# 128 background weight tiles: their loads move from SyncE's DMA queue to GpSimd's

## The reference, cut to what matters

```
shift, scale, gate = split(silu(cond) @ ada_w[i] + ada_b[i], 3)      # for c and for c_ctx
h = rmsnorm(x, norm_w[i]) * (1 + scale) + shift
layer 0: q, k, v, g = h @ gla_w_in ; gated linear attention ; y = (rmsnorm(o) * silu(g)) @ gla_w_out
layer 1: q, k, v, g = h @ diff_w_in ; differential softmax attention ; y = (...) @ diff_w_out
x = x + gate * y
```

## Time and profile before

| | |
|---|---|
| median of 3 runs | 1594.27 us (1589.72 to 1596.06) |
| the profiled execution, its own time | 1593.43 us |
| its span, first to last instruction | 1591.5 us |
| mean granted TensorE clock | 0.993 of full speed |
| PE busy | 1551.6 us, 97% |
| DVE busy | 1162.1 us, 73% |
| ACT busy | 606.0 us, 38% |
| POOL busy | 2.2 us |
| DMA of SP's queue (q1) | 256.55 MB, 50.3% of 16 engines' span |
| DMA of ACT's queue (q10) | 11.22 MB, 2.3% |

### The profile page before, as it was taken

The page is one execution under the profiler, slowest core; times in us unless marked ns, Lnnn a source line. Parts: engine busy times, 40 slices in busy tenths (PEclk is TensorE's granted clock), DMA queues, the critical chain, the costliest instruction groups (busy, mean ns, idle before and its releaser), DMA issues.

```text
span 1591.5 us, 19504 instructions
## 1 busy us (share of the span) xinstructions
PE 1551.6 (97%) x7602; PEld 1252.6 (79%) x7602; DVE 1162.1 (73%) x1799; ACT 606.0 (38%) x934; POOL 2.2 (0%) x9
## 2 busy tenths in 40 slices
PE   5999999999999999999999999999999999999998
PEld 3567888788888878788887778888888888888886
DVE  4444878887787789677887687777676768575865
ACT  4222434433444433542222444343333424243642
POOL 0000000000000000000000000000000000000000
PEclk9899999999999999999999999999999999999999
DMA  9996344554544464344876244445444444352554
GB/s 351 370 320 215 120 139 133 177 162 118 171 136 151 114 221 147 106 132 156 263 235 214 85 139 159 158 145 178 153 138 157 157 160 148 103 170 78 159 179 143
DMA packets 177352, 269.02 MB, mean 169 GB/s; under 512 B 12534, under 2 KB 111024, under 8 KB 176588
## 3 DMA queue, kind: packets, MB, share of 16 engines
q1 hardware_dynamic: 170464, 256.55, 50.3%
q10 hardware_dynamic: 6796, 11.22, 2.3%
HBM read 265.60 MB, written 2.12 MB: 168 GB/s over the span
## 4 chain that ended last, share of the span: by engine, by line
PE 81%; DVE 10%; DMA 4%; ACT 2%; issue 1%; SPq 0%; ACTq 0%; DVEq 0%
PE bank L1172 62%; PE bank L1636 5%; DVE ada_w L1689 3%; DMA ada_w<-in_ada_w 3%; PE bank L1353 2%; PE bank L1104 2%; DVE w_lo L1664 2%; PE bank L1256 1%; PE bank L1257 1%; PE bank L1258 1%; DMA u<-in_ctx 1%; DVE work L1959 1%; ACT w_hi L641 1%; PE bank L1215 1%; DMA u<-in_ada_w 1%
## 5 line engine op out<-in xcount | busy, mean ns | idle before, releaser
L1172 PE MATMUL bank<-w_lo,acts_hi 128*128 128x512 f32 x1536 | 606.5, 395 | 12.5 <-DVE acts_lo L2088 3.4
L1172 PE MATMUL bank<-w_hi,acts_lo 128*128 128x512 f32 x1536 | 599.1, 390 | 0.0
L1172 PE MATMUL bank<-w_hi,acts_hi 128*128 128x512 f32 x1536 | 598.9, 390 | 0.0
L641 ACT ACTIVATE w_hi<-w_raw 128x1024 fp32r<-128x1024 f32 (+1 forms) x296 | 304.1, 1034 | 592.0 <-PE bank L1172 510.2
L1664 DVE TENSOR_TENSOR w_lo<-w_raw,w_hi 128x1024 fp32r<-128x1024 f32 (+1 forms) x296 | 349.8, 1192 | 175.4 <-ACT w_hi L641 175.0
L1172 PEld LDWEIGHTS bank<-w_lo,acts_hi 128*128 128x128 f32 x1536 | 288.8, 188 | 84.5 <-issue 12.9
L1172 PEld LDWEIGHTS bank<-w_hi,acts_lo 128*128 128x128 f32 x1536 | 288.7, 188 | 61.0
L1172 PEld LDWEIGHTS bank<-w_hi,acts_hi 128*128 128x128 f32 x1536 | 288.8, 188 | 57.2
L1689 DVE SCALAR_TENSOR_TENSOR ada_w<-ada_w,silu_p 128x1024 f32<-128x1024 f32 x210 | 261.5, 1280 | 36.7 <-DMA ada_w<-in_ada_w 34.0
L1172 PE MATMUL bank<-acts_hi,w_lo 128*128 128x512 f32 x208 | 83.6, 402 | 1.1 <-DVE acts_lo L1789 1.1
L1172 PE MATMUL bank<-acts_lo,w_hi 128*128 128x512 f32 x208 | 81.6, 392 | 0.0
(11 more groups left out here) (227 smaller groups left out, 1514.9 us busy)
## 6 DMA issues: line engine op xcount, KB each, us to landing
ada_w<-in_ada_w SPq DMA_DIRECT2D x146, 512.0 KB, 4.5
w_raw<-in_diff_w_in SPq DMA_DIRECT2D x256, 256.0 KB, 3.1
w_raw<-in_gla_w_in SPq DMA_DIRECT2D x64, 512.0 KB, 4.2
w_raw<-in_gla_w_out SPq DMA_DIRECT2D x32, 512.0 KB, 4.9
w_raw<-in_diff_w_out SPq DMA_DIRECT2D x32, 512.0 KB, 4.4
u<-in_ada_w SPq DMA_DIRECT2D x24, 512.0 KB, 9.4
w_raw<-in_gla_w_in SPq DMA_DIRECT2D x40, 256.0 KB, 3.5
w_raw<-in_gla_w_in SPq DMA_DIRECT2D x48, 128.0 KB, 4.1
```

The lines of the kernel that those rows point to most:

```text
L641: act.activation(w_hi[:, s, :, 0:w], raw[:, s, :, 0:w], ACT.Copy).then_inc(w_hi_ok, 1)
L1172: last = pe.matmul(bank[b][:], a, w, start=(k == 0 and i == 0), stop=(k == NK - 1 and i == 2))
```

## The change

All 128 `modulation_tile` requests leave SP's program and are issued by GpSimd, after its five memsets, one after the other, with the same waits, the same tiles, the same buffers and the same semaphores. SP keeps the layer-0 start-up loads of `ada_w` (line 473) and all pairs.

```
--- before.py
+++ after.py
@@ -473,18 +473,6 @@   (on SP)
-            def modulation_tile(m):
-
-                i, k = m // NK, m % NK
-                layer, part = ((0, 2), (1, 0), (1, 1), (1, 2))[i // 2]
-                if m < 2:
-                    sp.wait_ge(ada_used, QUADS)
-                else:
-                    sp.wait_ge(weighed, m - 1)
-                first = part * D + i % 2 * HALF_COLS
-                sp.dma_start(ada_tile[:, m % 2], io["ada_w"][layer][k * P:(k + 1) * P, first:first + HALF_COLS])\
-                    .then_inc(tile_in[m % 2], 16)
-
@@ -536,9 +524,6 @@   (on SP, in load_chunk)
-                    for m in range(WEIGHS):
-                        if c * PAIRS + p == (6 if m < 2 else WEIGH_AT[m - 2]):
-                            modulation_tile(m)
@@ -624,6 +609,21 @@   (on GpSimd, after its memsets)
+            def modulation_tile(m):
+
+                i, k = m // NK, m % NK
+                layer, part = ((0, 2), (1, 0), (1, 1), (1, 2))[i // 2]
+                if m < 2:
+                    pool.wait_ge(ada_used, QUADS)
+                else:
+                    pool.wait_ge(weighed, m - 1)
+                first = part * D + i % 2 * HALF_COLS
+                pool.dma_start(ada_tile[:, m % 2], io["ada_w"][layer][k * P:(k + 1) * P, first:first + HALF_COLS])\
+                    .then_inc(tile_in[m % 2], 16)
+
+            for m in range(WEIGHS):
+                modulation_tile(m)
```

## The result

The changed kernel takes 1599.83 us (median of 12 runs, 1597.34 to 1601.60) against 1593.09 (12 runs). The medians differ by 6.7 us; the ratio of the two sets of runs is 1.0046, 95% interval 1.0038 to 1.0053, that is 7.3 us more (6.1 to 8.4), and this is the figure used from here on. The prediction said 1602.9 us in a range of 1593 to 1618, and slower with a chance of 0.55. Time and sign are right, though by the prediction's own bound of 0.5%, 8.0 us, a loss of 7.3 us would still have been called "same". The working is not right: the lateness is a third of what I took, its price is about twice what my formula gives, and about half of it is paid where I saw cover. The profiled execution took 1598.33 us, 4.9 more than before's, so its trace shows about two thirds of the loss.

What follows compares the result with a forecast made beforehand. PE, busy 97%, was taken as the bound, with DVE the bound in five stretches where late tile landings reach PE. At d = 1.1, 1.1 + 2.2 + 3.1 + 1.1 + (0.9 + 2.2 - 2.0) = 8.6 us, forecast 1602.9 us, range 1593 to 1618.

Steps and rivals of the forecast that it cites:

- formula: Sum over five stretches where PE waits through DVE: 9d - 2.2 up to d = 0.8, above that 12d - 4.6.
- likeliest case: The forecast itself: d from 0.7 to 1.8, centre 1.1, time 1598 to 1612 us; chance 0.50.
- nearly hidden: Rival: d below 0.7, so -2.2 to +4.1 us, time 1592 to 1598; chance 0.20.
- d: Added time from the end of weigh(m - 2) to the landing of tile m; taken as 1.1 us, ends 0 and 4.1.
- The steps covered in `OUT0` and layer 1: `OUT0` before 835 us and layer 1: delay hidden by `low` running ahead and by DVE's idle time; no cost.
- 2d and 3d between the heads: 264 to 288 us: two late landings, 2d (2.2 us); 566 to 593 us: three, 3d - 0.2 (3.1 us).
- The own queue's 2.0 us at 847.86 us: Third chunk of `OUT0`: the 8.38 us tile passes a weight load ahead of it on SP's queue; -2.0 us.
- 189 to 211 and 620 to 641 us: Decays of head 0 and of head 3: one late landing on the chain each, d (1.1 us) apiece.
- Held up by DVE: Rival: GpSimd's request waits for DVE's current instruction to end; d = 2.3, 23.0 us, time 1617; chance 0.22.
- Nothing to pay for 128 requests on SP: Taking 128 requests, 43.5 us, off SP is worth nothing, since SP would have waited for the next `low` anyway.
- weights not late: Pairs land as before; the opposing rival had some 25 layer-0 pairs 0.3 us late, 8 us on top, 1611; chance 0.03.
- 5.6 us in all: PE's total wait in between its busy stretches, taken as the most an own queue could give back.

Runs made afterwards that it cites:

- slope's kernel: The changed kernel, with GpSimd clearing 512 columns of the free buffer ahead of each request; 1617.44 us, +24.4 against before.
- kernel of layer 1 alone: The kernel before, but the 30 tiles from 98 on are requested by GpSimd; 1593.82 us, +1.6 against before.
- the one with lateness on SP's queue: The kernel before, SP still requesting, but each request waits until GpSimd has cleared 384 columns of the free buffer; 1597.3 us, +4.1.
- the ring of four: The kernel before, its two tile buffers used as four half tiles of 512 columns, requested by SP, weighed half by half; 1587.09 us, ratio 0.9967.

## Why the prediction was right, point by point

The time came out inside the likeliest case (1598 to 1612), but of two errors that cancel, which is luck: by the measured lateness the case is the rival "nearly hidden" (d below 0.7, chance 0.20), whose time was 1592 to 1598. The table has the prediction's formula at the lateness that was measured, and the steps of PE's matmuls against those of before, in us:

| stretch (us of before) | formula, d = 0.33 | changed kernel | formula, d = 1.06 | slope's kernel |
|---|---|---|---|---|
| start, to 160 | 0 | +0.7 | 0 | +0.4 |
| 189 to 211 | 0.3 | -0.6 | 1.1 | 0.0 |
| 264 to 291 | 0.7 | +0.8 | 2.1 | +3.8 |
| 291 to 550 | 0 | 0 | 0 | +1.2 |
| 566 to 597 | 0.8 | +1.2 | 3.0 | +7.0 |
| 620 to 642 | 0.3 | -0.6 | 1.1 | -1.6 |
| 755 to 797 | 0 | +2.2 | 0 | +9.5 |
| 845 to 960 | -1.3 | +0.8 | 0.9 | +1.2 |
| layer 1 | 0 | +0.4 | 0 | +2.3 |
| sum | 0.8 | 4.9 | 8.1 | 23.8 |

The first row is not the change's: it arises ahead of 53 us, and the first tile is requested at 145 us.

- **The size of d** was the first error. I took 1.1, the middle between two rows of ACT's queue, and it is 0.33 (0.25 at the median). By the test that the prediction set itself, a median from request to landing that moves less than 0.4 (it went from 4.3 to 4.2), this step was wrong. The rows of ACT's queue held something else: the longer of them, 4.9 us, were loads amid a burst, and probably it was the burst that made them long. The Trainium skill's figures for the first byte ("DMA: Bandwidth & Descriptors", "Latency and other measured facts") gave 0.4 between the two paths; the packets show 0.22 to 0.26 from the request, and 0.5 with the later start. Either would have been the better choice.
- **The steps covered in `OUT0` and layer 1** were the second. The step that failed reads: "In `OUT0` before 835 us PE doesn't wait at all, since `low` runs up to four pairs ahead." PE not waiting shows that it has slack, not how much, and `low` is not all that PE takes from DVE. At line 1119 it waits for `weighed`, with 1.45 us to spare. A page of waits shows such an edge only once it is crossed. In the changed kernel this is the largest step, 2.2 us, and with tiles 67 to 82 undelayed the slope's kernel loses 6 to 8 us less. Not all of the 2.2 may be the change's: the kernel of layer 1 alone, with before's code there, is 0.7 us late at the same place in its execution. Layer 1, "a burst of up to four late tiles costs 4d = 4.4 us, which that idle time takes", crossed a smaller edge: 0.5 to 0.6 us at 1309 us, by traces alone, and so PE does wait in layer 1, which the prediction had named as a sign of being wrong. From 290 to 550 us the cover held at 0.33 us; at 1.06, close to the d = 1.1 that it was said to bear, it gave way by 1.2 us, 1.0 of it at 497 us.
- **2d and 3d between the heads** were too small in slope. At 1.06 us the steps are 3.8 and 7.0 in place of 2.1 and 3.0. Of these, 1.6 and 2.1 us are the clock behind the wait, which the prediction did not price; that leaves 2.2 and 4.8, so nearly 2 us of the second come from elsewhere, and I did not take them apart.
- **The own queue's 2.0 us at 847.86 us** did not come. The chain's tile there takes 8.48 us after, 8.38 before. It was not the weights ahead of it in line that made it slow, as the prediction thought it might be; a tile by GpSimd is slow amid the same loads. The same holds at 757.72 us (8.65): SP's request of that tile took 7.57 us before, 8.12 in the kernel of layer 1 alone and 8.73 in the one with lateness on SP's queue.
- **189 to 211 and 620 to 641 us** shrank instead of growing by d each. The second shrinks by 0.6 to 1.6 us in every kernel that I ran, by 1.4 in that of layer 1 alone, whose code is before's there, so it is no gain of the change; rather the profiled run of before was long there. The first goes from -0.9 to +0.7 us among the kernels and stands at +0.7 in that of layer 1 alone, so a d of 0.3 can't be seen in it; why it shows nothing at 1.06 us I leave open.
- **Held up by DVE** (0.22) was rightly second choice, and does not happen: 527 ns at the median, and a landing 0.1 us longer beside a `low` than without one (medians). With one-input instructions it would, at some requests. The 14 of line 1687 that the prediction names met none of the requests.
- **Nothing to pay for 128 requests on SP, and weights not late:** right. Behind the start-up no wait of PE or DVE names w_raw.
- **The waits of DVE for tiles** went up by 10 us, not 40, which is d again. PE still has no wait from 290 to 550 us: right.
- **"5.6 us in all"** was a misreading of PE's waits from 160 to 960 us. The same view holds 6.2 us more, 5.9 of it in these two lines, all behind 900 us at the change to layer 1:

```profile
PE bank L1172 <- DVE acts_lo L2088: 3.4, 2, 1.9
...
PE bank L1172 <- DVE v_lo L2174: 2.5, 1, 2.5
```

So 5.6 us was no bound on what an own queue could give back. And the 2.5 us take up lateness of PE: in the changed kernel they shrink to 1.0 (see the last section).

## What to carry to other kernels

Ask of a moved request not only what the queues do but how late the landing is behind what frees its buffer, and count how often such landings stand in series: the chain of the changed kernel passes fifteen where it passed eight, and at 16 to 23 us for a microsecond 0.3 us became 7. Where PE doesn't wait, measure its distance to each thing that it takes from the late engine, the sums as well as the weights, before calling a delay hidden. And when a double buffer makes an engine wait at every turn, cut the same memory into more and smaller pieces: here it removed three quarters of the wait, and with it nearly all of the difference that the requesting queue made.

## What the hardware showed that I had not expected

- GpSimd's request comes later in two parts. It starts 0.30 us behind the end of the weigh at the median, and at every sixth request 0.54, where SP's starts after 0.03. Its first packet follows after 1.24 us, where SP's takes 0.98. Its transfers were 0.19 us shorter in the mean.
- Behind a wait of PE the clock may or may not be granted at half, with the same wait: at the 1.90 us for line 2088 (915 us of before) the matmuls behind it stayed at 0.39 us before (granted clock 1.00 from 915 to 920 us) and went to 0.63 for 3 us after (0.57 from 920 to 924 us of its own time); at the 2.5 us for line 2174 (946 us) they stayed at 0.39 before and went to 0.63 in the ring of four. Each such time puts PE back by about 1.6 us. It need not cost the kernel that: in the changed kernel the wait for line 2174 that follows is 1.5 us shorter for it (1.0 in place of 2.5). So of the +0.8 us of the table for 845 to 960 us 0.7 is the step at 870 us. Where no such wait follows, a part of the scatter between runs (1590 to 1596 us of one kernel) may be this; that was only argued.
- A one-input DVE instruction of 0.68 us stretched some of GpSimd's requests to 1030 ns, and the landings beside it took 0.56 us longer at the median than those without one.
